# Feed-forward gate and up with one moving operand of 512 columns: the upper weight part times both parts of x

## The reference, cut to what matters

```
D_MODEL = 1024
SEQ = 256
D_FF = 2816

def swiglu(x, w_gate, w_up, w_down):
    return (jax.nn.silu(x @ w_gate) * (x @ w_up)) @ w_down

x = x + 0.5 * swiglu(rmsnorm(x, ffn1_norm[l]), ffn1_w_gate[l], ffn1_w_up[l], ffn1_w_down[l])
```

## Time and profile before

| | before |
|---|---|
| median of 3 runs | 2869.95 us (2867.29 to 2869.97) |
| the profiled execution | 2867.51 us, span 2865.7 us |
| TensorE busy (PE) | 2683.1 us, 94% of the span |
| weight loads (PEld) | 2365.6 us, 83% |
| VectorE busy (DVE) | 1906.5 us, 67% |
| ScalarE busy (ACT) | 1420.0 us, 50% |
| moved by DMA | 601.79 MB, mean 210 GB/s |
| matmuls at L430 (gate and up) | 3 x 1760 |
| matmuls at L445 (down, with two operands of the feed-forward) | 3 x 472 |

### The profile page before, as it was taken

How to read it: one execution, slowest core, us unless ns; L and a number is a source line. 1 busy time by engine, 2 the same in 40 slices (tenths; PEclk the granted TensorE clock), 3 DMA queues, 4 the chain that set the end, 5 groups by cost and what they waited for, 6 DMA issues and landing times.

```text
span 2865.7 us, 49715 instructions
## 1 busy us (share of the span) xinstructions
PE 2683.1 (94%) x20030; PEld 2365.6 (83%) x20048; DVE 1906.5 (67%) x1722; ACT 1420.0 (50%) x1330; POOL 79.7 (3%) x82
## 2 busy tenths in 40 slices
PE   8999989999999989986999987999999999999997
PEld 7988888989988779976998986787777777787775
DVE  5456765555455855555546754788888888888786
ACT  4344513334344514343335733566766666666665
POOL 6000005000000000000000000000000000000000
PEclk9999999999999999997999999999999999999999
DMA  7564213555553305542555400899999999999995
GB/s 270 190 197 133 94 47 119 189 176 162 185 187 118 109 18 164 187 154 88 191 184 154 152 28 9 300 339 345 345 337 342 337 339 340 337 339 328 327 343 195
DMA packets 343044, 601.79 MB, mean 210 GB/s; under 512 B 12000, under 2 KB 180832, under 8 KB 342752
## 3 DMA queue, kind: packets, MB, share of 16 engines
q1 hardware_dynamic: 335264, 590.84, 60.7%
q10 hardware_dynamic: 7616, 8.58, 0.9%
HBM read 598.34 MB, written 1.05 MB: 209 GB/s over the span
## 4 chain that ended last, share of the span: by engine, by line
DMA 51%; PE 26%; DVE 11%; ACT 7%; DVEq 2%; issue 1%; SPq 1%; another core or an unknown queue 0%; ACTq 0%; PEldq 0%; PEld 0%; POOLq 0%
DMA raw<-in_moe_w_up 26%; DMA raw<-in_ffn_w_down 19%; DVE wlo L296 7%; ACT whi L293 6%; PE ps L430 5%; PE ps L792 5%; DMA raw<-in_dn_w_in 4%; PE ps L445 3%; DMA raw<-in_w_in 2%; PE ps L676 2%; PE ps L392 1%; DMA raw<-in_pool_w_in 1%; PE ps L1160 1%; PE ps L1147 1%; PE ps L1156 1%
## 5 line engine op out<-in xcount | busy, mean ns | idle before, releaser
L296 DVE TENSOR_TENSOR wlo<-raw,whi 128x2048 fp32r<-128x2048 f32 x562 | 1286.5, 2289 | 607.5 <-ACT whi L293 605.3
L293 ACT CAST whi<-raw 128x2048 fp32r<-128x2048 f32 x562 | 1071.6, 1908 | 677.5 <-DMA raw<-in_ffn_w_down 177.4
L430 PE MATMUL ps<-xhi,whi 128*128 128x256 f32 x1760 | 500.2, 284 | 3.2 <-DVE xlo L380 3.2
L430 PE MATMUL ps<-xlo,whi 128*128 128x256 f32 x1760 | 498.7, 283 | 0.0
L430 PE MATMUL ps<-xhi,wlo 128*128 128x256 f32 x1760 | 498.6, 283 | 0.0
L2499 PE MATMUL ps<-whi,xhi 128*128 128x512 f32 x896 | 365.3, 408 | 7.6 <-remote 5.6
L2499 PE MATMUL ps<-wlo,xhi 128*128 128x512 f32 x896 | 350.1, 391 | 2.9 <-issue 2.9
L2499 PE MATMUL ps<-whi,xlo 128*128 128x512 f32 x896 | 350.4, 391 | 0.0
L430 PEld LDWEIGHTS ps<-xhi,whi 128*128 128x128 f32 x1760 | 338.4, 192 | 5.8 <-DVE xlo L380 3.4
L430 PEld LDWEIGHTS ps<-xhi,wlo 128*128 128x128 f32 x1760 | 338.3, 192 | 1.9
L430 PEld LDWEIGHTS ps<-xlo,whi 128*128 128x128 f32 x1760 | 338.3, 192 | 0.0
(11 more groups left out here) (499 smaller groups left out, 3733.3 us busy)
## 6 DMA issues: line engine op xcount, KB each, us to landing
raw<-in_moe_w_gate SPq DMA_DIRECT2D x112, 1024.0 KB, 5.2
raw<-in_moe_w_up SPq DMA_DIRECT2D x112, 1024.0 KB, 5.5
raw<-in_moe_w_down SPq DMA_DIRECT2D x112, 1024.0 KB, 5.0
raw<-in_ffn_w_gate SPq DMA_DIRECT2D x55, 1024.0 KB, 5.1
raw<-in_ffn_w_up SPq DMA_DIRECT2D x55, 1024.0 KB, 5.1
raw<-in_ffn_w_down SPq DMA_DIRECT2D x55, 1024.0 KB, 4.8
raw<-in_w_in SPq DMA_DIRECT2D x24, 1024.0 KB, 5.1
raw<-in_dn_w_in SPq DMA_DIRECT2D x16, 1024.0 KB, 5.6
```

The lines of the kernel that those rows point to most:

```text
L293: act.copy(whi[:, n % SPLIT, 0:width], raw[:, n % RAW, 0:width]).then_inc(hi_ready[n % SPLIT], 1)
L296: dve.tensor_tensor(wlo[:, n % SPLIT, 0:width], raw[:, n % RAW, 0:width], whi[:, n % SPLIT, 0:width], ALU.subtract).then_inc(split_ready[n ...
L430: mm = pe.matmul(dst[:, b * ntok:(b + 1) * ntok], w[:, n % SPLIT, c * GW + b * P:c * GW + (b + 1) * P], xt[part][:, c, 0:ntok], start=(c = ...
```

## The change

The two parts of x become one tensor, `xboth`, in which the 256 columns of the upper part and the 256 of the lower part of a chunk lie one behind the other; `xhi` and `xlo` are views of it. In `wide`, the upper weight part is multiplied by both in one matmul of 512 columns (8 chunks), then the lower weight part by the upper part of x in matmuls of 256 columns (8 chunks) that add to the first half of the same bank. A block now fills one bank: gate takes banks 4 and 5, up takes 6 and 7, in every group. The two halves of a bank are summed later: ScalarE copies the second halves to memory, VectorE adds the first halves, for gate and for up; silu and product then work from memory.

VectorE's refills move one place on: gate sum, refill for the gate slot, up sum and hidden values, refill for the up slot, and the refill for the down slot comes first in the next pass. The refill at the start of a stage moves behind the first gate sum; the last one of a stage moves into `add_y`, behind the first of its four additions.

```diff
--- before.py
+++ after.py
@@ -189,8 +189,8 @@
         raw = sb("raw", [P, RAW, TILE])
         whi = sb("whi", [P, SPLIT, TILE], F32R)
         wlo = sb("wlo", [P, SPLIT, TILE], F32R)
-        xhi = sb("xhi", [P, C, S], F32R)
-        xlo = sb("xlo", [P, C, S], F32R)
+        xboth = sb("xboth", [P, C, 2, S], F32R)
+        xhi, xlo = xboth[:, :, 0, :], xboth[:, :, 1, :]
         hhi = sb("hhi", [P, 2, 2, S], F32R)
         hlo = sb("hlo", [P, 2, 2, S], F32R)
         work = sb("work", [P, WORK])
@@ -229,6 +229,9 @@
         tile_done = [sem(f"tile_done{i}") for i in range(SPLIT)]
         hid_ready = [sem(f"hid_ready{i}") for i in range(2)]
         hid_made = sem("hid_made")
+        gate_summed = sem("gate_summed")
+        gate_copied = sem("gate_copied")
+        up_copied = sem("up_copied")
         hid_turned = sem("hid_turned")
         hid_hi = sem("hid_hi")
         go = {k: sem(f"go_{k}") for k in ("pe", "dve", "act")}
@@ -401,6 +404,7 @@
                 pe.sem_clear(f["xt_ready"])
 
         FFN_BANK = 4
+        GATE_BANK, UP_BANK = 4, 6
 
         def project_bank(n):
             return 2 * (n % SPLIT)
@@ -419,19 +423,27 @@
         def take_split(pe, n):
             take(pe, split_ready[n % SPLIT])
 
-        def wide(pe, n, dst, ntok, xt, fresh=False):
+        def wide(pe, n, first_bank, fresh=False):
 
             take_split(pe, n)
             for b in range(2):
                 for c in range(C):
                     if fresh and b == 0:
                         wait_xt(pe, c)
-                    for k, (w, part) in enumerate(PASSES):
-                        mm = pe.matmul(dst[:, b * ntok:(b + 1) * ntok],
-                                       w[:, n % SPLIT, c * GW + b * P:c * GW + (b + 1) * P],
-                                       xt[part][:, c, 0:ntok], start=(c == 0 and k == 0),
-                                       stop=(c == C - 1 and k == 2))
+                    pe.matmul(ps[:, first_bank + b, :], whi[:, n % SPLIT, c * GW + b * P:c * GW + (b + 1) * P],
+                              xboth[:, c].rearrange("p a t -> p (a t)"), start=(c == 0), stop=False, skip_group_check=True)
+                for c in range(C):
+                    mm = pe.matmul(ps[:, first_bank + b, 0:S], wlo[:, n % SPLIT, c * GW + b * P:c * GW + (b + 1) * P],
+                                   xhi[:, c, :], start=False, stop=(c == C - 1), skip_group_check=True)
             return mm
+
+        def two(v):
+            return v.rearrange("p (b t) -> p b t", b=2)
+
+        def two_parts(first_bank):
+
+            v = ps[:, first_bank:first_bank + 2, :].rearrange("p b (a t) -> p b a t", a=2)
+            return v[:, :, 0, :], v[:, :, 1, :]
 
         def down(pe, n, hp, nt, last, banks=(0, 1, 2, 3), made="y_part", fresh=False, opened=lambda i: None):
 
@@ -472,30 +484,34 @@
             return tuple([h[:, q, b, :] for b in range(2)] for h in (hhi, hlo))
 
         def ffn_tensor(pe, n, groups, nt=TT, after_norm=True):
-            ntok = nt * P
-
-            def gate_up(m, q, fresh=False):
-                wide(pe, m, ps[:, 4 + q, :], ntok, (xhi, xlo), fresh).then_inc(tile_done[m % SPLIT], 1)
-                wide(pe, m + 1, ps[:, 6 + q, :], ntok, (xhi, xlo)).then_inc(tile_done[(m + 1) % SPLIT], 1)
+            def gate_up(m, fresh=False):
+                wide(pe, m, GATE_BANK, fresh).then_inc(tile_done[m % SPLIT], 1)
+                wide(pe, m + 1, UP_BANK).then_inc(tile_done[(m + 1) % SPLIT], 1)
 
             def step(m, q):
-                gate_up(m, q)
+                gate_up(m)
                 take(pe, hid_ready[1 - q])
                 down(pe, m + 2, hidden(1 - q), nt, False)
 
-            gate_up(n, 0, after_norm)
+            gate_up(n, after_norm)
             open_y(pe, 2 * nt)
             ffn_steps(pe, n + 2, groups, step)
             q = (groups - 1) % 2
             take(pe, hid_ready[q])
             down(pe, n + 3 * groups - 1, hidden(q), nt, True)
 
-        def ffn_scalar(act, n, groups, nt=TT):
-            w = 2 * nt * P
+        def ffn_scalar(act, n, groups):
 
             def gate(m, q):
                 take(act, tile_done[m % SPLIT])
-                act.activation(sil[:, q, 0:w], ps[:, 4 + q, 0:w], ACT.Silu)
+                act.copy(two(sil[:, q, :]), two_parts(GATE_BANK)[1]).then_inc(gate_copied, 1)
+                split_hi(act, m + SPLIT)
+                take(act, gate_summed)
+                act.activation(sil[:, q, :], sil[:, q, :], ACT.Silu)
+
+            def up(m):
+                take(act, tile_done[m % SPLIT])
+                act.copy(two(hid), two_parts(UP_BANK)[1]).then_inc(up_copied, 1)
                 split_hi(act, m + SPLIT)
 
             def other(m):
@@ -504,45 +520,58 @@
 
             def step(m, q):
                 gate(m, q)
-                other(m + 1)
+                up(m + 1)
                 other(m + 2)
 
             gate(n, 0)
-            other(n + 1)
+            up(n + 1)
             ffn_steps(act, n + 2, groups, step)
 
-        def ffn_vector(dve, n, groups, nt=TT):
-            w = 2 * nt * P
-            ntok = nt * P
+        def ffn_vector(dve, n, groups):
+
+            def add_hi(dst, first_bank):
+                return dve.tensor_tensor(two(dst), two_parts(first_bank)[0], two(dst), ALU.add)
 
             def refill(m):
                 take(dve, hi_ready[m % SPLIT])
                 split_lo(dve, m)
 
-            def hid_group(q):
-
-                dve.tensor_tensor(hid[:, 0:w], ps[:, 6 + q, 0:w], sil[:, q, 0:w], ALU.mult)
+            def gate_sum(q):
+                take(dve, gate_copied)
+                add_hi(sil[:, q, :], GATE_BANK).then_inc(gate_summed, 1)
+
+            def up_sum():
+                take(dve, up_copied)
+                add_hi(hid, UP_BANK)
                 dve.drain()
-                hv = hid[:, 0:w].rearrange("p (b t) -> p b t", b=2)
-                dve.tensor_copy(hhi[:, q, :, 0:ntok], hv)
+
+            def make_hidden(q):
+                dve.tensor_tensor(hid, hid, sil[:, q, :], ALU.mult)
                 dve.drain()
-                dve.tensor_tensor(hlo[:, q, :, 0:ntok], hv, hhi[:, q, :, 0:ntok],
-                                  ALU.subtract).then_inc(hid_ready[q], 1)
+                dve.tensor_copy(hhi[:, q], two(hid))
+                dve.drain()
+                dve.tensor_tensor(hlo[:, q], two(hid), hhi[:, q], ALU.subtract).then_inc(hid_ready[q], 1)
 
             def step(m, q):
+                refill(m - 1 + SPLIT)
+                gate_sum(q)
                 refill(m + SPLIT)
+                up_sum()
+                make_hidden(q)
                 refill(m + 1 + SPLIT)
-                hid_group(q)
-                refill(m + 2 + SPLIT)
-
+
+            gate_sum(0)
+            refill(n + 2)
+            up_sum()
             refill(n + SPLIT)
-            refill(n + 1 + SPLIT)
-            hid_group(0)
+            make_hidden(0)
             ffn_steps(dve, n + 2, groups, step)
 
-        def add_y(dve, scale):
+        def add_y(dve, scale, after_first=lambda: None):
 
             for i, (t, s) in enumerate(PARTS):
+                if i == 1:
+                    after_first()
                 dve.wait_ge(f["y_part"], i + 1)
                 if i == len(PARTS) - 1:
                     dve.sem_clear(f["y_part"])
@@ -2802,9 +2831,8 @@
 
             def vector(dve, n, l):
                 norm_vector(dve, gain, FFN_BANK, known)
-                refill_vector(dve, n)
                 ffn_vector(dve, n, FG)
-                add_y(dve, scale)
+                add_y(dve, scale, lambda: refill_vector(dve, n + 3 * FG - 1))
                 return n + 3 * FG
 
             def scalar(act, n, l):
```

## The result

| | before | after |
|---|---|---|
| median of 4 runs, same chip | 2869.39 us (2867.29 to 2869.97) | 2844.23 us (2840.6 to 2847.9) |
| span of the profiled execution | 2865.7 us | 2838.8 us |
| ratio | | 0.9911, 95% interval 0.9899 to 0.9924 |

The change makes the kernel 25.2 us faster; 22.2 were forecast, and 2844.23 lies in the range of 2841 to 2856. In the profiled executions the difference is 26.9 us.

What follows compares the result with a forecast made beforehand. TensorE was taken to bound the five feed-forward stages, transfers the expert stage. Matmuls 21.3, beginnings -3.4 and ends 4.3 sum to 22.2 us saved: 2869.95 becomes 2847.8, range 2841 to 2856.

Steps and rivals of the forecast that it cites:

- Part 1: Gate and up tiles: 16 fewer matmuls save 12.1 ns each, 0.39 us a pass, 21.3 us over 110 tiles.
- Part 2: First block of each feed-forward stage: eight lower-weight matmuls come after the last chunk of x; 3.4 us lost in all.
- TensorE starts later behind the chunks: Three of five stage beginnings: with a late or half-clock start, the loss is 0.95, 0.48 and 0.29 us.
- the chunk working: First block: matmuls wait for x chunks 0.40 us apart, and eight of 0.12 us follow the last; 0.84 lost.
- Part 3: Stage ends: hidden values ahead of a refill remove TensorE's stall; 0.65 us at four ends, 1.7 at the fifth, 4.3 total.
- Part 4: Loop passes and first groups: added copies, adds and single-bank-pair waits are all covered; costed at nothing, bounds 0 to 3 us.
- Rival (a): Norms behind stage ends: longer idle drops the clock, 2.5 us each at one to three ends; 2850.3 to 2855.3; chance 0.22.
- (b): Gate and up: a 512-column matmul spaces like two of 119.9 ns, so no saving; 2869.0 us; chance 0.07.
- (c): Gate in every pass: TensorE waits for the single bank pair's refill; 58 us slower, 2928; chance 0.04.
- (d): Stage ends: all five give their whole gain, 4.2 us more, 2843.6 us; chance 0.07.
- 11.4 us, my 5.3 doubled: Gate's copy, sum and refill chain: the length beyond which the single bank pair would stall TensorE every pass.

Runs made afterwards that it cites:

- the kernel with the refill first: Changed kernel with a stage's last refill ahead of the first of the four additions to x instead of behind it; 2852.56 us, ratio 0.9943.
- The first-block kernel: Changed kernel with each chunk's lower-weight matmul right behind its 512-column matmul in the first block of a stage's first tile; 2842.11 us, ratio 0.9912.

## Why the prediction held

**Part 1, the matmuls: right, a little large.** A pass lost 0.366 us where 0.39 was forecast, so the tile's 16 dropped matmuls are worth 11.4 ns each, not 12.1: those of 512 columns stand 230 ns apart in gate and up, not the 227.7 of down. 55 groups x 0.366 = 20.1 us against 21.3. Undoing it alone gave 19.3 back, with the beginnings in it. The Trainium skill, page "TensorE: Matmul & The Clock Gate", section "Wait — 56ns, not 53.3ns?", has 2.5 ns on top per warm matmul; these runs show 13 to 17, so the estimate by the page (4.4 us) was off and the rows of down were the right neighbour.

**Part 2, the beginnings: right sum, wrong parts.** Forecast 0.95 for the program's start, 0.84 for each ffn2, 0.48 for ffn1 in layer 1 and 0.29 for ffn3. Measured (what the first gate and up didn't gain of their 0.366): 0.96 and 0.95 for ffn2, but 1.05 for ffn1 in layer 1 and 1.02 for ffn3, while the program's start won 0.35 on top. Together 3.6 against 3.4. The step that failed is "TensorE starts later behind the chunks", which stood on slow norms ahead of two of these stages: 6.06 and 6.31 us in the kernel before, from the norm's first matmul to the stage's first gate matmul. In the changed kernel's profiled execution they took 3.60 and 5.40, and all four beginnings took 12.94 to 12.97 us. Where such a norm was slow and the first block the same, the step held: in the kernel with the refill first, ffn1 in layer 1 took 12.52 behind a norm of 5.22, and ffn3 12.19 behind one of 6.46, losses of 0.61 and 0.27 (ahead of ffn3 the 5.40 us of the changed kernel weren't slow enough for that). So the chunk working was right, and which beginning is short goes with the clock in the norm ahead of it, which an execution of before can't tell. The 0.35 of the program's start is the spread of executions, as far as is known: it took 13.18 to 14.28 us in the four kernels with this first block. The first-block kernel, at 12.12 to 12.15, shows that the lower-weight matmuls behind the last chunk are the loss.

**Part 3, the ends: the right mechanism, sized too small.** 8.0 us against 4.3, still inside its bounds of 1 and 8.5. Two terms were off. The four ordinary ends won 1.06, 1.05, 1.11 and 0.96 instead of 0.65: I let the last refill start 0.31 us behind its cast, and it starts 0.14 behind it (199.73 to 199.87), as before; and I carried the gap of 0.37 us between refill and additions over from the earlier trace rows, and after the change it is 0.14 (202.16 to 202.30). Together that is the 0.4 missing. And the text said that the hidden values gain 1.7 and the refill takes most of it back; the kernel with the refill first shows what each is worth: TensorE's earlier start alone 0.23 (14.72 to 14.49), the place of the last refill 0.83. The fifth end, the layer boundary, won 3.81 and another 2.46 in its norm, where I took 1.7: the "issue" wait was named in the earlier trace rows as if it were independent of VectorE's order, and it left with that order.

**Part 4, the added work: right.** No wait in a pass of the loop, even with the copies made five times.

**The sum.** The profiled executions differ by 26.9 us, 4.7 more than the 22.2 forecast. The ends gave 3.7 more than forecast, and the norms another 3.7 that the forecast didn't have: 2.46 at the boundary, the rest in the pooling stage's norm, which took 4.99 to 6.55 us in the twelve executions whatever the kernel. The stages gave 1.5 less (16.4 against 17.9), and all else lost 1.2.

**Rival (a), the clock falls at the ends: it exists, and that it stayed away here was luck.** In the changed kernel's profiled execution the four norms behind idle times of 2.44 to 2.60 us ran at 1.00, the upper of the two levels (2.4 GHz). (The forecast had 2.98; its own terms, 1.90 + 1.70 - 0.65, give 2.95.) In four other kernels with such ends they didn't always. All norms behind feed-forward stages, by the idle time of TensorE before them, one profiled execution of each kernel and two of the kernel before:

| idle before the norm | slow norms (4.9 to 6.6 us against 3.56 to 3.60) | kernels |
|---|---|---|
| 0.2 to 0.4 us, behind zero matmuls | 0 of 8 | 2 |
| 1.68 to 1.92 us | 1 of 12 | before (twice) and 2 like it |
| 2.44 to 2.94 us | 8 of 20 | changed and 4 with VectorE's new order |
| 3.26 to 3.42 us | 4 of 4 | refill first |
| 4.40 to 4.67 us | 4 of 4 | before (twice) and 2 like it |
| 9.59 to 12.47 us (pooling) | 12 of 12 | all |

The norms behind the last mixer, not in the table, were slow in 12 of 12 behind 3.26 to 3.29 us. So the rival's price was right in kind (1.4 to 1.6 us for a slow norm behind 2.44 to 2.94 us, 2.5 forecast). That it can belong to an execution and not to a kernel is shown by the two executions of the kernel before, 3.57 and 5.19 us for one norm behind 1.90 and 1.91 us. How much of the 7 us between the changed kernel's fastest and slowest run it explains isn't shown; the kernel with the zero matmuls alone still spreads by 4.4. The Trainium skill, same page, section "Why this matters for your kernels", warns of idle gaps between bursts of matmuls. The counts above agree that longer gaps are slow more often, but not that a gap's length alone decides: between 2.44 and 2.94 us the same gap did both.

**Rivals (b), (c) and (d).** (b) fell with the 230 ns, (c) with the five copies. (Its "11.4 us, my 5.3 doubled" was a slip: the cover worked out was 11.0, and 5.3 doubled is 10.6.) (d), "the ends give all", had the better sum (8.5) for another reason: four ends gave about 1.05 and one 3.8.

**Outside of the parts.** Two differences repeat. The pooling stage takes 67.9 to 68.1 us in all seven kernels with the changed gate and up, 65.0 to 65.8 in the five without; VectorE's row in the changed kernel:

```profile
1296.08 0.69 DVE L1758 TENSOR_TENSOR work<-work 128x512 f32<-128x512 f32 x1 [3.19 <-issue]
```

And all after the norm behind ffn3 takes 1315.3 to 1319.1 us in the seven, 1323.1 to 1325.7 in the five; of the stalls that the kernel before has there, "[2.89 <-issue]" at 2604.78 is one, at 2.32 to 2.89 us in the five and in none of the seven. Neither follows the merging (undone, both stay), VectorE's order, the layout or the one shift of VectorE's program that was tried. What the seven share is the copies and additions and the one pair of banks; that these do it is only what is left over, not shown.

## What to carry to other kernels

Read the spacing of starts at the full clock, not durations: where it carries a fixed part per matmul (13 to 14 ns here), widening the moving operand pays by the count of matmuls dropped, and a pass of before gives the sum within a tenth. When a refill stands at the end of a stage, ask which squaring or norm step it delays, and how long TensorE idles for it: 0.83 us more at each of five ends made the kernel 8.3 us slower, because the clock fell as well. A few matmuls on zeros into a free bank cover such a gap at no cost on the path (the ends stayed at 13.7 us, and 0 of 8 norms were slow); what they won alone, 2.5 us, isn't told apart from nothing.

## What was not expected of the hardware

- The same norm of the same kernel behind the same idle time (1.90 and 1.91 us) ran at the upper clock in one execution and slowly in another; behind 2.44 to 2.94 us 8 of 20 norms were slow.
- A wait for issue on TensorE of 4.40 to 4.67 us in four executions of kernels with the old order of VectorE is gone in all eight with the new one, though TensorE's program had not changed in one of them; neither the place of the last refill nor a last down tile 1.1 us late brings it back. A wait put down to issue isn't always a matter of the engine's own program.
- 39 memsets and drains at the start cost 8.2 us, of which 2.35 are seen where they stand.
